# Modulation sums: four groups of weight units share one turn, and the token loads wait for them

## The reference, cut to what matters

```python
sh_l, sc_l, g_l = jnp.split(jax.nn.silu(c) @ w_mod[l] + b_mod[l], 3, axis=-1)
sh_c, sc_c, g_c = jnp.split(jax.nn.silu(c_ctx) @ w_mod[l] + b_mod[l], 3, axis=-1)
hl = xl * (1.0 + sc_l[:, None, :]) + sh_l[:, None, :]
hc = xc * (1.0 + sc_c) + sh_c
parts_l = jnp.split(hl @ w_in[l], SPLIT_POINTS, axis=-1)   # conv, attention and pooling branches
...                                                        # attention over context and tokens
xl_new = _layernorm(DEEPNORM_ALPHA * xl + g_l[:, None, :] * out_l, ln_g[l], ln_b[l])
```

## Time and profile before

| what | value |
|---|---|
| median of three runs | 3008.71 us |
| the profiled execution | 3009.78 us, of which 3008.1 us are the span from first to last instruction |
| TensorE matmul busy | 2931.9 us of the span (97%) |
| VectorE, ScalarE busy | 1814.5 us (60%), 1308.4 us (43%) |
| chain that ended last | TensorE 90%, VectorE 5%, ScalarE 2%, DMA 1% |
| mean granted TensorE clock | 0.989 |
| DMA | 523.17 MB, mean 174 GB/s; 368 GB/s in the first fortieth of the span, 298 in the second |

### The profile page before, as it was taken

One profiled execution on the slowest core, in us unless ns is written; L12 is line 12 of the kernel. 1 busy time (PEld: TensorE's weight loads), 2 busy tenths in 40 slices (PEclk: granted clock), 3 DMA queues, 4 the chain that ended last, 5 costly groups with the idle time before them and its releaser, 6 DMA issues.

```text
span 3008.1 us, 41185 instructions
## 1 busy us (share of the span) xinstructions
PE 2931.9 (97%) x15214; PEld 2393.1 (80%) x15214; DVE 1814.5 (60%) x2937; ACT 1308.4 (43%) x2003; POOL 99.0 (3%) x156
## 2 busy tenths in 40 slices
PE   6899999999999899999998999999999999999998
PEld 3677777777777688888786888888888888888886
DVE  2255455454644546777786577778877656565564
ACT  2242233232332434444556544445655545354453
POOL 0000010101000001110100000000000000000000
PEclk8999999999999999999999999999999999999999
DMA  9744343434354423343353444444555555555453
GB/s 368 298 157 168 141 166 145 166 142 168 140 192 189 179 98 126 141 146 137 138 194 126 183 161 175 158 177 156 192 183 196 189 189 188 199 185 196 182 195 126
DMA packets 76146, 523.17 MB, mean 174 GB/s; under 512 B 8800, under 2 KB 11360, under 8 KB 13920
## 3 DMA queue, kind: packets, MB, share of 16 engines
q1 hardware_dynamic: 71872, 509.64, 45.3%
q0 software_dynamic: 2688, 8.91, 0.8%
q10 hardware_dynamic: 1440, 2.60, 0.2%
HBM read 519.02 MB, written 2.10 MB: 173 GB/s over the span
## 4 chain that ended last, share of the span: by engine, by line
PE 90%; DVE 5%; ACT 2%; DMA 1%; issue 1%; SPq 0%; DVEq 0%; POOLq 0%; ACTq 0%; POOL 0%
PE bank L1770 24%; PE bank L1773 12%; PE bank L1760 9%; PE bank L1761 9%; PE bank L1762 9%; PE bank L2101 4%; PE bank L2102 4%; PE bank L2103 4%; PE bank L1794 3%; PE bank L1796 3%; PE bank L1795 3%; PE bank L1805 3%; DVE w_lo L1058 2%; DMA raw<-stream 1%; PE bank L1902 1%; PE bank L1937 1%
## 5 line engine op out<-in xcount | busy, mean ns | idle before, releaser
L1058 DVE TENSOR_TENSOR w_lo<-raw,w_hi 128x1024 fp32r<-128x1024 f32 x776 | 937.8, 1224 | 632.6 <-ACT w_hi L572 630.7
L572 ACT ACTIVATE w_hi<-raw 128x1024 fp32r<-128x1024 f32 x776 | 814.7, 1056 | 778.0 <-DMA raw<-stream 343.7
L1760 PE MATMUL bank<-x,w_hi 128*128 128x512 f32 x1120 | 443.6, 396 | 1.5 <-DVE x L1109 0.8
L1761 PE MATMUL bank<-x,w_hi 128*128 128x512 f32 x1120 | 436.4, 390 | 0.0
L1762 PE MATMUL bank<-x,w_lo 128*128 128x512 f32 x1120 | 436.3, 390 | 0.0
L584 ACT ACTIVATE z<-bank 128x512 f32<-128x512 f32 x256 | 153.2, 598 | 432.5 <-PE bank L1773 272.1
L1770 PE MATMUL bank<-xs,w_hi 128*128 128x512 f32 x1184 | 304.8, 397 | 0.8 <-DVE xs L1109 0.8
L1760 PEld LDWEIGHTS bank<-x,w_hi 128*128 128x128 f32 x1120 | 210.2, 188 | 82.7 <-issue 40.9
L1770 PE MATMUL bank<-mlp_x,w_hi 128*128 128x512 f32 x1024 | 257.1, 393 | 0.0
L1762 PEld LDWEIGHTS bank<-x,w_lo 128*128 128x128 f32 x1120 | 210.3, 188 | 45.0
L1770 PEld LDWEIGHTS bank<-xs,w_hi 128*128 128x128 f32 x1184 | 213.0, 189 | 41.0 <-DVE xs L1109 2.2
(11 more groups left out here) (292 smaller groups left out, 3540.3 us busy)
## 6 DMA issues: line engine op xcount, KB each, us to landing
raw<-stream SPq DMA_DIRECT2D x484, 1024.0 KB, 4.8
res<-tokens POOLq DMA_DIRECT2D x8, 512.0 KB, 8.6
work<-tokens POOLq DMA_DIRECT2D x16, 256.0 KB, 7.1
out<-res SPq DMA_DIRECT2D x8, 256.0 KB, 3.4
gain_sb<-final_gain ACTq DMA_DIRECT2D x1, 1024.0 KB, 8.0
table_sb<-tables ACTq DMA_DIRECT2D x1, 640.0 KB, 3.5
pool_sb<-pool_w POOLq DMA_DIRECT2D x8, 64.0 KB, 4.4
work<-lam_in ACTq DMA_DIRECT2D x1, 256.0 KB, 4.6
```

What stands on the lines that cost most here:

```text
L572: own.inc(act.activation(w_hi[:, 2 * unit.parity + g, :], raw[:, unit.slot, g * HALF:(g + 1) * HALF], ACT.Copy), hi_done, 2 * unit.number ...
L1058: own.inc(dve.tensor_tensor(w_lo[:, n, :], raw[:, unit.slot, g * HALF:(g + 1) * HALF], w_hi[:, n, :].bitcast(F32), ALU.subtract), lo_done, ...
L1760: pe.matmul(bank[:, :], hi, tile(k)[:, 0, :], start=k == 0, stop=False)
L1761: pe.matmul(bank[:, :], hi, tile(k)[:, 1, :], start=False, stop=False)
```

## The change

A turn now serves several groups. There are 8 turns: turns 0 to 3 take two groups each (8 units, the shift and the scale of one `kq`), turns 4 to 7 four groups each (16 units). To keep the groups apart in one bank, the stationary operand becomes a *window* of 32 columns in a row of 38: the two condition columns stand at 6 and 7, and group i of a turn reads columns 6-2i to 37-2i, so that its sums come out in rows 2i and 2i+1 of each 32. `chooser` has 8 columns, so one collect of four matmuls serves all groups of a turn; `modulation` writes up to 16 columns at once (two instructions), and in turns 0 to 3 two ranges of four columns (four instructions).

In the first stretch TensorE no longer collects after the first four units of a `kq`; ScalarE and VectorE split unit 2kq-1 ahead of the turn's copy, not inside it. The token loads, unrolled, wait besides for `mod_mm`: loads 0 and 1 until two modulation units are multiplied, 2 and 3 until ten, 4 and 5 until 18, 6 and 7 until 26.

Beside the products the turns end at units 29, 45 and 61. Turn 7 is begun at unit 62 and holds `gemm_bank[1]` until layer 1's values, so its last four units are multiplied in that bank too; unit 75's product goes to `att[5]` instead, and the first value group of layer 1 uses `gemm_bank[0]` instead of `gemm_bank[1]`. The waits that guarded the old assignment are changed with it.

```diff
+SHARE = 4
+TURNS = 8
...
+def mods_before(turn):
+    return 8 * turn if turn < 4 else 32 + 16 * (turn - 4)
+
+def mod_rows(u):
+    turn = u // 8 if u < 32 else 4 + (u - 32) // 16
+    first, last = mods_before(turn), mods_before(turn + 1) - 1
+    return turn, (u - first) // 4, first, last
...
-        cond_x = place("cond_x", [KT, SQUARE])
-        chooser = place("chooser", [2])
+        cond_x = place("cond_x", [KT, SQUARE + 2 * (SHARE - 1)])
+        chooser = place("chooser", [2 * SHARE])
...
-        v_banks = [[att[2:6], [*att[0:2], gemm_bank[1], att[2]]], [[*att[3:6], gemm_bank[1]], att[0:4]]]
+        def product_bank(unit):
+            return att[5] if unit.fixed == PAIRS + 1 else gemm_bank[unit.bank]
+        v_banks = [[att[2:6], [*att[0:2], gemm_bank[1], att[2]]], [[*att[3:6], gemm_bank[0]], att[0:4]]]
...
-            pool.dma_start(res[:, 0:2, :], tokens[:, 0:2, :]).then_inc(tok_in, 16)
-            with pool.Fori(0, KT // 2 - 1) as i:
-                pool.wait_ge(tok_in, 16 * i + 16)
-                ahead = bass.ds(2 * i + 2, 2)
-                pool.dma_start(res[:, ahead, :], tokens[:, ahead, :]).then_inc(tok_in, 16)
+            for i in range(KT // 2):
+                if i:
+                    pool.wait_ge(tok_in, 16 * i)
+                pool.wait_ge(mod_mm, 8 * (i // 2) + 2)
+                pool.dma_start(res[:, 2 * i:2 * i + 2, :], tokens[:, 2 * i:2 * i + 2, :]).then_inc(tok_in, 16)
...
-            def take_mod(group, b):
-                act.wait_ge(mod_mm, 4 * group + 4)
-                own.inc(act.activation(z[:, b, :], gemm_bank[b][:, :], ACT.Copy), modz_full, group + 1)
+            def take_mod(turn, b, row):
+                act.wait_ge(mod_mm, mods_before(turn + 1))
+                own.inc(act.activation(z[:, row, :], gemm_bank[b][:, :], ACT.Copy), modz_full, turn + 1)
...
             for kq in range(4):
-                for b in range(2):
-                    take_mod(2 * kq + b, 0)
-                    if kq and b == 0:
-                        split(Unit(2 * kq - 1))
-                act.wait_ge(mod_done, 2 * kq + 2)
+                if kq:
+                    split(Unit(2 * kq - 1))
+                take_mod(kq, 0, 0)
+                act.wait_ge(mod_done, kq + 1)
...
-                    if l == 0 and unit.fixed > PAIRED and unit.fixed % 4 == 1:
-                        take_mod(8 + (unit.fixed - PAIRED) // 4, 1)
+                    if l == 0 and unit.fixed > PAIRED and (unit.fixed - PAIRED) % 16 == 15:
+                        take_mod(4 + (unit.fixed - PAIRED) // 16, 1, 1)
...
-            def modulation(group, m, b):
-                dve.wait_ge(mod_sum, group + 1)
-                for s in range(2):
-                    last = dve.tensor_tensor(mod[:, bass.ds(m, 4), s],
-                                             gemm_bank[b][:, 0:8].rearrange("p (m s) -> p m s", s=2)[:, :, s],
-                                             vec[:, bass.ds(VEC_COLS["b_mod"] + m, 4)], ALU.add)
+            def modulation(turn, b, places):
+                dve.wait_ge(mod_sum, turn + 1)
+                sums_at = gemm_bank[b][:, 0:8 * SHARE].rearrange("p (c g s) -> p g c s", c=4, s=2)
+                for m, first, n in places:
+                    for s in range(2):
+                        target = mod[:, m:m + 4 * n, s].rearrange("p (g c) -> p g c", c=4)
+                        bias = vec[:, VEC_COLS["b_mod"] + m:VEC_COLS["b_mod"] + m + 4 * n]
+                        last = dve.tensor_tensor(target, sums_at[:, first:first + n, :, s],
+                                                 bias.rearrange("p (g c) -> p g c", c=4), ALU.add)
...
             for kq in range(4):
-                for b in range(2):
-                    modulation(2 * kq + b, 4 * kq + KT * b, 0)
-                    if kq and b == 0:
-                        split(Unit(2 * kq - 1))
+                if kq:
+                    split(Unit(2 * kq - 1))
+                modulation(kq, 0, [(4 * kq, 0, 1), (KT + 4 * kq, 1, 1)])
...
             def mod_product(u, b):
                 place, q = mod_place(u), u % 4
+                turn, group, first, end = mod_rows(u)
+                window = slice(2 * (SHARE - 1 - group), 2 * (SHARE - 1 - group) + SQUARE)
...
-                    ins = pe.matmul(gemm_bank[b][rows, :], cond_x[:, 4 * q + j, :],
-                                    raw[:, place % RAW_SLOTS, WIDE * j:WIDE * (j + 1)], start=q == 0, stop=q == 3)
+                    ins = pe.matmul(gemm_bank[b][rows, :], cond_x[:, 4 * q + j, window],
+                                    raw[:, place % RAW_SLOTS, WIDE * j:WIDE * (j + 1)], start=u == first, stop=u == end)
-            def mod_collect(group, b):
-                pe.wait_ge(modz_full, group + 1)
+            def mod_collect(turn, b, row):
+                pe.wait_ge(modz_full, turn + 1)
                 for c in range(4):
-                    ins = pe.matmul(gemm_bank[b][:, 2 * c:2 * c + 2], z[:, b, P * c:P * (c + 1)], chooser[:],
+                    ins = pe.matmul(gemm_bank[b][:, 2 * SHARE * c:2 * SHARE * (c + 1)], z[:, row, P * c:P * (c + 1)], chooser[:],
                                     start=True, stop=True)
...
-                elif n % 4 == 2:
-                    pe.wait_ge(mod_done, group)
+                elif (n - PAIRED) % 16 == 0:
+                    pe.wait_ge(mod_done, turn)
                 mod_product(18 + n, 1)
-                if n % 4 == 1:
-                    return lambda: mod_collect(group, 1)
+                if (n - PAIRED) % 16 == 15:
+                    return lambda: mod_collect(turn, 1, 1)
...
             for kq in range(4):
+                if kq:
+                    pe.wait_ge(mod_done, kq)
                 for b in range(2):
-                    if kq + b:
-                        pe.wait_ge(mod_done, 2 * kq + b)
                     for q in range(4):
                         mod_product(8 * kq + 4 * b + q, 0)
                     if kq:
                         value_both(kq - 1, b, 0)
-                    mod_collect(2 * kq + b, 0)
+                    if b == 1:
+                        mod_collect(kq, 0, 0)
                     if kq:
                         value_both(kq - 1, b, 1)
...
-            pe.wait_ge(z_full, Unit(W_OUT0 + 14).taken + 1)
             for u in range(MODS - 4, MODS):
-                mod_product(u, 0)
+                mod_product(u, 1)
```

More of the change, by code:

```diff
@@ L579, in take @@
                 if unit.fixed == PAIRS + 1:
-                    act.wait_ge(mod_done, MOD_GROUPS - 1)
+                    act.wait_ge(mod_done, TURNS - 1)
                 elif not unit.early(V_UNITS[0] + 1):
                     act.wait_ge(z_used, unit.taken + 1 - unit.back)
+                source = product_bank(unit)
                 if gain is None:
-                    last = act.activation(z[:, unit.bank, :], gemm_bank[unit.bank][:, :], ACT.Copy)
+                    last = act.activation(z[:, unit.bank, :], source[:, :], ACT.Copy)
                 else:
@@ L587, in take @@
                         cols = slice(TOK * s, TOK * (s + 1))
-                        last = act.activation(z[:, unit.bank, cols], gemm_bank[unit.bank][:, cols], ACT.Copy,
+                        last = act.activation(z[:, unit.bank, cols], source[:, cols], ACT.Copy,
                                               scale=mod[:, 2 * KT + gain, s:s + 1])
@@ L810, in layer_out @@
                 for k in range(KT):
-                    if l == 0 and k % 4 == 1:
-                        take_mod(19 + k // 4, 1)
+                    if l == 0 and k == 1:
+                        take_mod(TURNS - 2, 1, 1)
                     if k == KT - 1:
@@ L1090, in _ @@
             own.wait_own()
-            own.inc(dve.tensor_tensor(cond_x[:, :, 0:2], cond_sb[:], cond_e[:], ALU.mult), cond_full, 1)
+            own.inc(dve.tensor_tensor(cond_x[:, :, 2 * (SHARE - 1):2 * SHARE], cond_sb[:], cond_e[:], ALU.mult), cond_full, 1)
             dve.wait_ge(vec_in, 16)
@@ L1096, in _, with later_modulation @@
             own.wait_own()
-            def modulation(group, m, b):
-                dve.wait_ge(mod_sum, group + 1)
-                for s in range(2):
-                    last = dve.tensor_tensor(mod[:, bass.ds(m, 4), s],
-                                             gemm_bank[b][:, 0:8].rearrange("p (m s) -> p m s", s=2)[:, :, s],
-                                             vec[:, bass.ds(VEC_COLS["b_mod"] + m, 4)], ALU.add)
-                own.inc(last, mod_done, group + 1)
+            def later_modulation(turn):
+                modulation(turn, 1, [(mods_before(turn), 0, SHARE)])
+            def modulation(turn, b, places):
[7 more added lines that the diff above has]
+                                                 bias.rearrange("p (g c) -> p g c", c=4), ALU.add)
+                own.inc(last, mod_done, turn + 1)
             def rest_tile(n, k, source, target, t):
@@ L1305, in after @@
                                 late_rest(k)
```

(22 more changed lines are left out.)

14 lines of the change are left out of this document (6 added, 8 removed).

## The result

The changed kernel takes 2994.32 us (median of four runs, 2993.1 to 2995.22); the kernel before took 3009.99 us on the same chips (3008.71 to 3013.21). The ratio is 0.9946, with a 95% interval of 0.9929 to 0.9963: 15.7 us faster by the medians, 11 to 21 by the interval. Forecast were 2995.3 us, in a range of 2990.0 to 3000.5.

A forecast was written before the change was run, and what follows sets the result against it. TensorE was taken to bound the kernel beside products, DMA and then a loop of waits the first stretch. Savings of 10.8 + 2.6 = 13.4 us took the median from 3008.71 to 2995.3 us, range 2990.0 to 3000.5.

The forecast's parts named there:

- Collects beside products: Beside layer 0's products: twelve collects saved at 0.90 us of TensorE each, 10.8 us gained.
- Modulation products, banks, sums: Stationary loads from shifted windows, bank changes and late turns' sums: each taken to cost nothing.
- rival C: Modulation products' stationary loads: off-grid windows load slowly, 0.65 us more a unit, about 3043 us in all; chance 0.04.
- rival D: Collects: one of eight columns costs four times 0.90 us, so 10.8 us gained becomes about 0, 3006 us; chance 0.03.
- term (c): First stretch: a turn's sums take four instructions instead of two, four times; 0.7 us lost.
- First stretch: Before layer 0's products beside modulation: four terms, 1.6 + 2.7 - 0.7 - 1.0, together 2.6 us gained.
- rival B: First stretch pays more: 6.3 us there, 17.1 in all, 2991.6 us; chance 0.10.
- (a): First stretch: fewer token bytes ahead of modulation unit 11's load, which arrives earlier; 1.6 us gained, bounds 0 and 3.
- (b): First stretch, kq 1 to 3: the collect inside the first value group goes, 3 x 0.90 = 2.7 us gained.
- (d): First stretch: delayed token loads slow critical loads by a seventh, 0.5 us in each of two passes, 1.0 us lost.

The follow-up runs named there:

- e4: The kernel before with the four matmuls of each of the 15 collects beside products issued twice: 3024.47 us, ratio 1.0044.
- e1: The changed kernel with token loads no longer waiting for modulation units: 2996.67 us, ratio 0.9958 to the kernel before.
- e2: The kernel before with only the token loads' wait for modulation units added: 3007.88 us, ratio 0.9989.
- e8: The changed kernel run once more, unaltered, for a second trace: 2994.51 us in one execution.
- e3: The changed kernel with the first stretch as before, turns shared only beside products: 2998.65 us, ratio 0.9961 to the kernel before.
- e7: The kernel before with only weight units 1, 3 and 5 split ahead of the turn's copy and sums: 3013.45 us in one execution.
- e10: The kernel before with only weight units 0, 2, 4 and 6 split early: 3000.86 us, ratio 0.9965.
- e6: The changed kernel with weight units 0, 2, 4 and 6 split early: 2985.38 us, ratio 0.992 to the kernel before.

## Why the prediction was right, and where not

**Collects beside products: right.** 10.8 forecast, 11.3 measured (0.95 each; 0.89 for an added one). The 0.06 us between adding and removing one are open; the changed kernel's window also holds the bank changes, which e4 doesn't have.

**Modulation products, banks, sums: right.** The load's median is 109 ns as before, wherever the window starts, so rival C has fallen; the Trainium skill's statement in "TensorE: Matmul & The Clock Gate", "LDWEIGHTS (loading the stationary operand)", that the number of columns is what counts, agrees with that, though not its figure (27 ns for 32 columns by its formula). A collect of 8 columns is as long as one of 2 (median 256 and 251 ns), so rival D has fallen too. Four sums take 0.38 us instead of 0.24: term (c), four times 0.14, was 0.6 and not 0.7.

**First stretch: the sign and most of the mechanism right, the size wrong.** 2.6 forecast, 5.0 and 5.9 measured, close to rival B's 6.3. Term by term:
- (a) tokens against weights, 1.6: the two traces of the changed kernel show -0.6 and +1.9 at unit 11, the gate alone +1.4. In the second trace the load is down to 4.80 us, as the term said for fewer bytes; in the first it took 6.67. But the term also had the chain to that load start earlier. It didn't, with a load issued at 36.47 and 35.85 us (35.94 before), since turn 0's last unit and collect ran at half clock in both traces, 1.7 us longer together.
- (b) 2.7 for three collects: 4.8 and 2.8 in all. The second pass shows 14.68 to 13.68 us from unit 19 to 20, as said; in the second trace it shows nothing, since more of these products ran at half clock.
- (d) is the step that failed: "I take 0.5 us lost for each of two passes, 1.0". The gated token loads cost the critical loads nothing that can be seen: in the second pass 4.81, 4.75 and 4.66 us with one beside them, 4.78 in e1 without; in the third 5.79, 5.45 and 5.48 with, 5.48 in e1 and 5.58 before without. And the second pass's load became 1.4 us shorter, which isn't the gate's doing alone, since it is so in e1 too.
- Not in the forecast at all: the half clock after each wait. In the first trace passes 1 and 3 gained 1.1 and 0.9 us beyond their collect (1.99 and 1.76 us in all), and at pass 1 it can be counted in the chain. Over all three passes it gave 2.1 us beyond the collects in the first trace, 0.1 in the second and 1.6 in e1, so it is no steady part of the surplus; the row with term (d) is.

Why the token load cost nothing can be read from the DMA queues. Term (d) let it take its seventh from the moment of its issue. It was issued at 72.59 us, beside the critical load (72.00 to 76.81); its first packet moved 4.1 us later, when that load had all but landed. The queues from 72.59 to 76.6 us, then from 76.6 to 81:

```profile
q1 hardware_dynamic: 173, 1.29, 93.4%
```

```profile
q1 hardware_dynamic: 176, 1.31, 71.4%
q0 software_dynamic: 144, 0.52, 29.5%
```

In the second trace of the changed kernel and in e2 the packets begin 4.1 and 4.0 us after the issue too, and in the third pass of the three traces 0.6 to 1.2 us before the critical load has landed. Where a whole token load did move beside a critical load, at 37.5 us in the first trace, that took 1.9 us longer than in the second (e8). The Trainium skill's rule of turns between queues ("DMA: Bandwidth & Descriptors", "Queues, rings and completion order") would, at equal shares, have cost 1.2 us in each pass; these passes don't test that, since almost nothing of the token load was there to take turns with.

Why the second pass's load is short with the gate alone (4.66) and with the shared turns alone (4.78), and long in before, e3, e4 and e7 (6.23, 7.06, 7.36, 7.18), is not settled: it accounts for 1.3 to 1.6 us that each edit brings and both bring once. The late split as its cause was tested and has fallen. What the traces do show is the state of the DMA engines before it: in the four kernels with the long load they are full in the last whole microsecond ahead of its issue (share 0.95 to 1.03), in the five traces with a short one they are not (0.02 to 0.51). That goes with the difference; no run changes it alone. This microsecond before (load issued at 73.21) and in the changed kernel (72.00):

```profile
72.00:73.00 1.00, 0.77 (x12) 0.16 (x8) 1.00 (x2) 0.97 (x3) 0.00 (x0) 1.00 0.97 410
```

```profile
71.00:72.00 1.00, 1.00 (x14) 0.10 (x6) 0.97 (x1) 0.97 (x3) 0.00 (x0) 1.00 0.02 8
```

**What hid the error.** The profile that the forecast was built on lacks a spell of half clock at the start of layer 1's output projection that every other trace has: the window between the means of the two layers is 563.1 us in it, 565.1 and 565.2 in the two of the changed kernel, 564.8 to 566.1 in e2, e3, e4, e7 and e10, four of which have the turns of before. So these 2 us are no cost of the change. The forecast of 13.4 met 14.6 because the first stretch paid 2.4 us more and the window 0.5 more than said, and this spell took 2.0. That the two numbers lie so close is luck in that part; the collects beside products are not.

## What to carry to other kernels

Where one engine is busy without a gap, count its instructions and price them from two neighbours in the timeline; that came out within 6%. Where a loop of waits sets the pace, look at what the engine does ahead of the step that frees a buffer for the next load: moving that step, here the split, ahead of work that didn't need it was worth 12 us in the first stretch, more than removing instructions there. Two edits to such a loop may remove the same wait, so try each alone before adding up their gains.

## What the runs showed of the hardware

- A 1 MB load at the same place of the same kernel took 6.67 us in one execution and 4.80 in another. Across the kernels the loads on the chain behind turn 0 ranged from 4.7 to 9.3 us.
- A 512 KB token load from GpSimd's queue moved its first packet 3.4 to 4.4 us after its issue in 86 of 96 cases (eight loads in each of twelve traces; 72.59 to 76.65 us in the changed kernel), and 1.2 to 2.8 us after it in the other ten (36.25 to 37.49). So one that was issued together with a critical weight load of 4.8 us hardly shared its time.
- After one and the same wait of TensorE (2.0 us, at the first unit of layer 1's output projection) the granted clock fell to half (1.2 GHz) in eleven traces, of both orders of turns, and not in the trace of before. Windows of the changed kernel, and then of before:

```profile
1484.00:1486.00 2.00, 2.00 (x10) 1.85 (x10) 2.00 (x2) 1.02 (x1) 0.00 (x0) 0.58 0.96 380
1486.00:1488.00 2.00, 2.00 (x7) 1.65 (x7) 1.77 (x4) 1.55 (x2) 0.00 (x0) 0.57 0.64 112
```

```profile
1499.90:1501.90 2.00, 2.00 (x14) 1.76 (x14) 1.95 (x2) 1.59 (x3) 0.00 (x0) 1.00 0.89 356
```

  It costs 1.6 us. In e2 such spells, here and at two other joints, left 1.1 us of span of the 4.3 gained in the first stretch.
- Shorter waits gave more than their length: in e6 TensorE waits 14.2 us for loads in the first 190 us, 9.2 less than in the changed kernel (23.4), and weight unit 12 begins 12.4 us earlier. Against the second trace of the changed kernel (20.4 and 168.1) it is 6.2 less waiting and 11.4 us.
